# Turning queries and keys four steps behind their making, with four sets of buffers, in a latent-attention layer

## The reference, cut to what matters

```
q  = (rmsnorm(cq, q_norm) @ w_q_up)  -> 16 heads x (64 + 32)
kv = (rmsnorm(ckv, kv_norm) @ w_kv_up) -> 16 heads x (64 key + 64 value)
qn = rmsnorm(q[..., :64]);  qr = rope(rmsnorm(q[..., 64:]))
kn = rmsnorm(kv[..., :64]); v = kv[..., 64:];  kr = rope(rmsnorm(kr)), shared by all heads
s  = qn . kn + qr . kr          # 512 queries x 768 keys, head size 96
p  = softmax(s * 96 ** -0.5);  out = p @ v
```

## Time and profile before

| | us |
|---|---|
| median of 3 runs (2371.92 to 2376.51) | 2374.63 |
| profiled execution, its own time | 2371.86 |
| span of the profiled execution | 2370.2 |
| PE busy | 2157.1 (91%) |
| DVE busy | 997.0 (42%) |
| ACT busy | 611.8 (26%) |
| POOL busy | 252.4 (11%) |

### The profile page before, as it was taken

One profiled execution on the slowest core, in us unless ns is written; L12 is line 12 of the kernel. 1 busy time (PEld: TensorE's weight loads), 2 busy tenths in 40 slices (PEclk: granted clock), 3 DMA queues, 4 the chain that ended last, 5 costly groups with the idle time before them and its releaser, 6 DMA issues.

```text
span 2370.2 us, 35650 instructions
## 1 busy us (share of the span) xinstructions
PE 2157.1 (91%) x14802; PEld 1288.6 (54%) x14802; DVE 997.0 (42%) x2437; ACT 611.8 (26%) x1293; POOL 252.4 (11%) x541
## 2 busy tenths in 40 slices
PE   5999989999798969999999999778889989998887
PEld 3896538996576933444444444467676433333322
DVE  4466655677775352222222224766663321121111
ACT  3244435335565220000000002455542200000000
POOL 0001000001233200000000000332221100000000
PEclk8999999999999988999999999799999999999999
DMA  8224711103000489999999997000017699999998
GB/s 278 89 72 178 249 41 54 54 19 125 1 2 1 144 325 388 391 392 402 398 390 392 404 401 259 0 1 1 1 49 264 243 426 415 421 421 421 420 420 332
DMA packets 110110, 550.04 MB, mean 232 GB/s; under 512 B 8159, under 2 KB 35567, under 8 KB 81022
## 3 DMA queue, kind: packets, MB, share of 16 engines
q1 hardware_dynamic: 102814, 525.21, 55.5%
q0 software_dynamic: 4864, 16.78, 3.1%
q10 hardware_dynamic: 2272, 5.77, 0.7%
HBM read 526.77 MB, written 20.97 MB: 231 GB/s over the span
## 4 chain that ended last, share of the span: by engine, by line
PE 75%; DMA 9%; DVE 8%; ACT 3%; issue 2%; SPq 1%; POOL 1%; DVEq 0%; ACTq 0%; POOLq 0%
PE PS L2619 14%; PE PS L2782 9%; PE PS L2632 7%; DMA AR<-in_w_exp_gate_dram 6%; PE PS L884 3%; PE PS L1086 3%; PE PS L1158 2%; PE PS L477 2%; PE PS L1999 2%; PE PS L2001 2%; PE PS L2000 2%; PE PS L865 2%; PE PS L2745 2%; DMA AR<-in_w_exp_down_dram 2%; PE PS L907 1%
## 5 line engine op out<-in xcount | busy, mean ns | idle before, releaser
L2782 PE MATMUL PS<-AR 128*64 128x512 f32 x1536 | 347.9, 602 | 32.1 <-DMA AR<-in_w_exp_gate_dram 19.3
L2619 PE MATMUL PS<-AR 128*64 128x512 f32 x1536 | 343.2, 599 | 3.0 <-DVE AR L2691 2.0
L2782 PEld LDWEIGHTS PS<-AR 128*64 128x64 f32 x1536 | 109.7, 138 | 243.4 <-issue 216.5
L2619 PEld LDWEIGHTS PS<-AR 128*64 128x64 f32 x1536 | 106.7, 137 | 214.8 <-issue 214.7
L2632 PE MATMUL PS<-AR 128*32 128x256 f32 x3072 | 175.7, 381 | 0.0
L972 DVE TENSOR_REDUCE AR<-PS 128x1 f32<-128x768 f32 (+1 forms) x160 | 135.6, 848 | 72.0 <-PE PS L854 39.0
L927 ACT ACTIVATE AR<-PS,AR 128x768 f32<-128x768 f32 (+1 forms) x160 | 130.4, 816 | 52.2 <-DVE AR L972 24.5
L2632 PEld LDWEIGHTS PS<-AR 128*32 128x32 f32 x3072 | 94.9, 110 | 76.2 <-issue 15.4
L884 PE MATMUL PS<-AR 128*128 128x128 f32 x800 | 120.5, 281 | 14.7 <-DVE AR L1145 8.4
L884 PEld LDWEIGHTS PS<-AR 128*128 128x128 f32 x800 | 95.3, 144 | 45.8 <-issue 27.9
L2662 ACT COPY AR<-PS 128x512 f32<-128x512 f32 x16 | 9.4, 586 | 395.3 <-PE PS L2586 395.3
(11 more groups left out here) (467 smaller groups left out, 4035.4 us busy)
## 6 DMA issues: line engine op xcount, KB each, us to landing
AR<-in_w_exp_gate_dram SPq DMA_DIRECT2D x64, 2048.0 KB, 19.0
AR<-in_w_exp_up_dram SPq DMA_DIRECT2D x64, 2048.0 KB, 18.6
AR<-in_w_exp_down_dram SPq DMA_DIRECT2D x63, 2048.0 KB, 18.1
AR<-in_w_ada_dram SPq DMA_DIRECT2D x30, 2048.0 KB, 12.2
AR<-in_w_in_dram SPq DMA_DIRECT2D x12, 1024.0 KB, 5.3
AR<-in_w_in_even_dram SPq DMA_DIRECT2D x9, 1024.0 KB, 5.3
AR<-in_w_out_dram SPq DMA_DIRECT2D x2, 2048.0 KB, 10.5
AR<-x_rows SPq DMA_DIRECT2D x8, 512.0 KB, 6.1
```

What stands on the lines that cost most here:

```text
L2619: t = pe.matmul(bank(b)[64 * q_:64 * q_ + 64, :], op, w[:, c, 512 * q_:512 * q_ + 512], start=(h == 0 and c == 0), stop=(h == 1 and c == 3 ...
L2782: m = pe.matmul(bank(b)[64 * q_:64 * q_ + 64, :], op, w[:, c, 512 * q_:512 * q_ + 512], start=(h == 0 and c == 0), stop=(h == 1 and c == 3 ...
```

## The change

Groups 1 to 3 get `LAG` 4 in place of 3, fourteen fill steps in place of thirteen, and a fourth set of buffers, which is added to `STM` as its sixth entry. Its 4 KB lie behind the query weights in the slot that later holds the second half of `w_out_odd`, so that load gets a wait for the last turn. Groups 2 and 3 begin one unit earlier (13 and 29), group 1 still at unit 0.

```
+        STM.append((AR[:, 203 * 256:203 * 256 + 512], AR[:, 203 * 256 + 512:203 * 256 + 896],
+                    AR[:, 203 * 256 + 896:204 * 256 + 768], AR[:, H0 + 4352:H0 + 4384]))
...
-        LAG, STEPS = [5, 3, 3, 3], [15, 13, 13, 13]
+        LAG, STEPS = [5, 4, 4, 4], [15, 14, 14, 14]
 
         def stm(gi, k):
-            return STM[k % 5 if gi == 0 else (10 * gi + k) % 3]
+            return STM[k % 5 if gi == 0 else (0, 1, 2, 5)[(10 * gi + k) % 4]]
...
-            elif gi == 1 and k < 3:
+            elif gi == 1 and k < 4:
                 e.wait_ge("full", "ut", 0, 9)
             else:
-                n = 10 * gi + k - 3
+                n = 10 * gi + k - 4
                 e.wait_ge("full", "ut", n // 10, n % 10)
...
-                    fills.setdefault(max(0, 16 * gi - 2 + i), []).append(("up", gi + 1, i))
+                    fills.setdefault(max(0, 16 * gi - (3 if gi else 2) + i), []).append(("up", gi + 1, i))
...
+                if key == ("outo", 1):
+                    Q.wait_ge("full", "ut", 3, 9)
                 if key == ("outo", 0):
                     Q.wait_ge("full", "pv", "o", 47)
```

## The result

| | us |
|---|---|
| before, median of 4 runs (2371.92 to 2376.51) | 2373.63 |
| changed, median of 4 runs (2337.94 to 2342.52) | 2340.15 |
| ratio, 95% interval | 0.9858, 0.9841 to 0.9875 |
| profiled execution, before and changed | 2371.86 and 2341.25 |

The account below looks back on a forecast made before the run. PE's turns waiting for POOL's rotation, 36.2 us, were taken as the bound. Groups 1 to 3 gain 12.5 + 11.5 + 10.9 = 34.9 us; with half a microsecond off for handovers, 2340 us, range 2329 to 2354.

Parts of the forecast that it names:

- The ring through POOL: Query step from PE's turn through ACT, DVE and POOL to the next turn, 6.74 us; LAG 4 lets it take two steps.
- What is late next: A ring over DVE and ACT, in two halves measured low part to low part; nine halves sum to 39.85 us in group 2.
- A: Half from an odd step to the even one, through DVE's sum of squares and ACT: 4.02 us, 4.43 with a query tile.
- B: Half from an even step to the odd one, through DVE's norms, copy and scaling: 4.85 us, 5.37 with query norms.
- the half put at 3.1: Group 1's eighth half, from an odd step to the even one, no sum of squares left: estimated at 3.1 us.
- put at 2.7: Last half of groups 2 and 3, without the values' product and the wait for bank 6: estimated at 2.7 us.
- The clock: PE's granted clock in the query stretches, 0.80 before, was taken as full; above 0.95 was the sign of being right.
- rival 2: PE's clock still drops in the query stretches, 3 to 4 us a group back: gain 24, time 2350; chance 13%.
- What follows: Everything behind the attention, `outo` and all later weights, moves as a whole, issued by one queue that waits for step 50.
- rival 3: The end does not follow: the stream of weights sets it by itself, time stays at 2374.6; chance 3%.
- Rivals 1 and 4: PE becomes the bound, time 2318, chance 5%; or POOL's ring closes over two steps as over one, 2383, 4%.
- The rule on the shared interface: POOL's products and DVE's norms could block one another in 12 query steps, up to 5 us; the sum left it out.

Follow-up runs that it names:

- group 1 early: Changed kernel with group 1's fill steps begun one unit earlier as well, four of them at unit 0: 2343.45 us, ratio 0.9872 against the kernel before.

## Why the prediction was right, and where it was off

- *The ring through POOL* was the bound, and it is the lag, not the sets, that opened it: the waits of the turns for POOL are gone, sets alone give 0.9997, a lag of five gives no more, and more work for POOL costs 1.7 us a tile before the change.
- *What is late next* was sized half by half: but for the dip of the clock, eight of nine halves in each group lie within 0.15 us. The two reorderings confirm what each half hangs on: moving ACT's logarithm shortens A from 3.88 to 3.31 us, moving DVE's scaling shortens B from 5.36 to 4.80.
- *A step that failed:* "I cost it at nothing; its cover is about 3 us". I looked only at the tile's own turn. POOL also spreads the reciprocals in order behind the products. The prediction called that copy "wanted two steps on", but PE takes it in the very step in which it stands, and there the cover was less than nothing: PE waits 4.4 us for it in five steps.

```profile
1590.71 0.45 POOL L3383 TENSOR_TENSOR AR<-AR 128x128 f32<-128x128 f32 x1
1591.11 0.29 POOL L1054 COPY AR<-AR 128x128 f32<-128x128 f32 x1
1591.45 0.87 PE L884 MATMUL PS<-AR 128*128 128x128 f32 x6 [0.91 <-POOL AR L1054]
```

  That is why the half put at 3.1 was 3.58, and the last one of groups 2 and 3, put at 2.7, was 3.55: with the copy moved they are 2.89 and 2.44. It cost 2.9 us in these three halves, and with 1.5 us more of POOL's work in a tile 13 to 17 us. The 3 us of cover were too many for the tile's own turn as well: in the last steps of a group 1.5 us more made turns wait.
- *A term that was missing:* group 1 now ends in step 15, and unit 16's scores in step 16 wait for tile 9's low part. With the 0.86 us of the added tile, the piece to group 2's first turn grew by 1.60, not 0.86. The row on PE's timeline:

```profile
1600.22 0.36 PE L852 MATMUL PS<-ROH,ROL 96*128 96x256 f32 x1 [0.72 <-DVE RXL L3304]
```

- *Two numbers of the working.* PE's own work in a key pair was put under 8 us; the trace of the kernel before has 8.16 busy in the pair from 1552.06 to 1561.51, and a pair that makes two query tiles holds 8.93 of 9.15 us in the changed kernel. PE is not the bound, but the cover is a fraction of the 0.9 us that the prediction gives it. And 2.0 + 1.5 + 1.2 behind the last turn is 4.7, not 4.65; 4.80 was measured.
- *The clock* came back as forecast, but for group 2 in one of two profiles: rival 2 in small, at 0.6 us.
- *What follows* moved as a whole, 601.6 and 601.5 us, so rival 3 is out, though the last experts do wait for weights (16.6 us of PE's waits for their gate weights). In the other profiles it is 600.8 to 604.4 us, with no relation to how early the attention ended. Rivals 1 and 4 did not happen: PE still waits 5.4, 4.4 and 2.8 us in the three largest groups of waits, and no turn waits for POOL.
- *The rule on the shared interface* (the Trainium skill, "SBUF — State Buffer", "Who interferes with whom"): the prediction says that no run shows such a block, but the traces do, before and after the change, and agree with the rule. In a key tile DVE's first product of the norm reads two SBUF operands and starts just behind POOL's copy:

```profile
1564.22 0.29 POOL L3360 COPY AR<-AR 128x128 f32<-128x128 f32 x1 [2.10 <-DVE AR L3313]
1564.27 0.26 DVE L3332 TENSOR_TENSOR AR<-AR 128x4 f32<-128x4 f32 x1
```

  It ends as the copy ends, after 0.26 us; without POOL beside it the same product takes 0.15 (at 1573.40). That is 0.1 us in 15 of 18 key tiles, the same in the kernel before. The block that the prediction feared, in the query tiles, stayed away: POOL's last product takes 0.45 us as in the earlier trace rows, and the one with the gain 0.73, as the 0.72 of the earlier trace rows. With POOL's extra work it came: a product of DVE's norm took 0.71 us in place of 0.42 (at 1650.83), and the spread 0.48 in place of 0.29 in the rows of that experiment.

- The agreement of 2340 with 2340.15 is partly luck. The sum of 34.9 was 1.3 us above the 33.64 measured; half a microsecond had been taken off it without a row, and the gain was taken from a median of 2374.63, which is 2373.63 with the fourth run. The medians of one kernel vary by as much between sets of runs (the changed kernel 2340.15 and 2341.45, the one before 2372.2 to 2374.6).

## What to carry to other kernels

When work is passed round engines that each run in order, find the ring, count in how many steps it must close, and size the next ring from the starts of the same instructions before promising the whole wait. A result wanted one step later costs a set of buffers and a longer ramp (here some 0.9 us a group for a tile made in a step of its own, and 0.7 where the last result came late for its first use). Here only the first step of lag, the one that broke the ring, paid. For an engine said to have slack, look at everything that stands behind the work in its queue, small copies above all, and ask who waits for those.

## What the runs showed of the hardware that was not expected

TensorE's clock fell to its lower level behind short idle times, and not every time. In the second profile of the changed kernel the third pair of key products at unit 0, behind 0.96 us of idle time, took 2.06 us, and in the first, behind the same, 1.13. With LAG 5 two such pairs were slow; with group 1 early all of them, three behind the same waits, stayed at 1.13 or below. Likewise the same stretch of the same kernel ran at a granted clock of 0.92 in one execution and 1.00 in another, which was worth 0.6 us in 40. So two profiles of one kernel, cut into the same pieces, tell more than their totals: the 203.5 and 204.5 us of the changed kernel are 1.6 us more in one place and 0.6 less in another.
